# A decoder step on one core: expert scoring with four blocks per matmul, and retention samples in groups of 32 partitions

## The chip, the cores and the metric

The kernel runs on one core of one Trainium2 chip. The metric is the time of one execution on the device in microseconds (us). Names: TensorE (PE, matmuls; its weight loads are PEld), VectorE (DVE), ScalarE (ACT), GpSimd (POOL), SyncE (SP, which only issues DMAs here). Data lies in SBUF (128 partitions); matmuls write PSUM (eight banks of 512 fp32 per partition).

## The reference

One layer of a hybrid decoder, for 512 prompt tokens and 8 samples of 8 new tokens each (576 tokens, width 2048). Cut to what the change touches:

```python
def retention_chunk(q, k, v, s, log_gamma):          # s: state (B, H, dk, dv)
    ...
    inner = jnp.einsum('bhid,bhjd->bhij', q, k) * decay[None]
    o = (jnp.einsum('bhij,bhjv->bhiv', inner, v)
         + jnp.einsum('bhid,bhdv->bhiv', q, s) * xi[None, :, :, None])
    s_new = (s * jnp.exp(log_gamma * C)[None, :, None, None]
             + jnp.einsum('bhjd,bhjv->bhdv', k * zeta[None, :, :, None], v))
    return o, s_new
...
def retention_mixer(q, k, v, gate, pos, s0, ret_norm_g):   # 4 heads of 256
    ...
    o = (o - mu) * lax.rsqrt(var + NORM_EPS)
    return jax.nn.silu(gate) * (o * ret_norm_g), s_new
...
def peer(h, peer_wq, peer_subkeys, peer_u, peer_v):  # 8 heads, 16384 experts, 16 chosen of each
    ...
        u = jnp.take(peer_u, expert, axis=0)
        act = jax.nn.gelu(jnp.einsum('thkd,td->thk', u, xb), approximate=False)
        vv = jnp.take(peer_v, expert, axis=0)
        return jnp.einsum('thk,thkd->td', g * act, vv)
```

Around it: the input projection, causal pooling of the other half of the channels, the output projection, attention over 256 memory tokens per sequence, and a final norm.

## The kernel before

Every large product is made of three fp32r matmuls, high x high, high x low and low x high. A piece of weights (128 x 1024 fp32, 512 KB) arrives in a raw buffer by a DMA from SP; ScalarE rounds it into the high part of a slot of `WS` (`high`, `high2`, line 896), GpSimd subtracts to get the low part (`low_part`, line 404), TensorE uses it. `WS` has four slots; semaphores count the chain: `raw0` to `raw3`, `hi_done`, `split_done`, `used`. The tokens' parts lie in `HL`. `projection` (line 521) has the weights stationary and tokens moving (288 or 320 columns). Order on each engine is the order of the code; there is no scheduler.

**Retention** (`retention`, four heads; the last outside the loop). A head has eight projection blocks of two slots each (`head_block`, blocks 0 to 7); work on the previous results stands between them. After block 5 TensorE forms the prompt scores (line 626) and one 64 x 64 matrix of the samples (line 629); after block 6 the outputs. There, for each half of the head's channels, the four prompt tiles (line 639), the samples' inner part (line 641), and per sample and half of dk a matmul with a 128 x 128 piece of the sample's state stationary and its eight tokens moving (line 645). Then the prompt state (line 650). The new sample states are formed with the masked keys `KM` (64 partitions, one mask per sample): `state(b)` (line 660) writes bank 4 or 5, VectorE adds it to the decayed state (line 1494) and frees the bank. Two stand before block 7, the others between its k blocks. The means over the channels (line 669) stand before block 7, the variances (line 683) behind it. ScalarE copies the outputs out of PSUM, stores the states, takes the root, and only then loads the next head's tables and states and evacuates its block 0. In the last head block 7 is the first part of the output projection (`out_early`, 14 of 16 k blocks), for which ScalarE and VectorE split the mixed activations meanwhile (`split_early`, `lows`, line 1423).

**Expert scoring.** 320 tokens are scored later, against all experts. For the last 256 tokens `tokens_first` (line 793) runs inside the loop over the eight query heads: each iteration has two query projections, then the scores of 1/8 of the experts, 8 pairs of blocks of 128 experts. The tokens (`HLG`) are stationary, two expert blocks move at once: 256 columns, 96 matmuls to a pair. Slots are refilled in halves of 512 columns (`used_q`, `hi_q`, `split_q`; GpSimd's half subtractions are line 428), and the loads come in the order 0, 2, 1, 3. ScalarE applies Gelu to 512 columns (`gelu_tokens`, line 1223) and stores them to `gelg`, from which GpSimd later gathers. VectorE meanwhile selects the top 16 of the query head (lines 1581 to 1625). After it a later stage scores the other tokens and multiplies by v, with rows of `vE` gathered.

## Time and profile before

| | us |
|---|---|
| median of 3 runs | 4879.75 |
| lowest, highest | 4876.03, 4882.84 |
| the profiled execution, as timed | 4868.53 |
| its span in the trace | 4866.4 |
| TensorE busy | 4551.1 |
| GpSimd busy | 3099.6 |
| VectorE busy | 2297.8 |
| ScalarE busy | 1584.6 |

The retention heads lie between about 390 and 980 us of the span, the query projections with the scoring of 256 tokens between 1750 and 2737 us. A row of the timeline gives the start, the length and the engine, the line, the operation, "written <- read" by the program's names, the shape, how many instructions were merged, and in brackets how long the engine was idle before and what ended that. Matmul times include the way through the array, so neighbouring ones overlap: the pace is read from the start of one row to that of the next, or from a count over a stretch. An fp32 matmul (not fp32r) shows as two instructions. [...]

### The profile page before, as it was taken

Reading aid. Unit: us, or ns where it says so; the run is one execution under the profiler, and the core shown is the slowest. Engines: PE = TensorE matmul, PEld = TensorE weight load, DVE = VectorE, ACT = ScalarE, POOL = GpSimd, SP = SyncE. Lnnn points to the kernel's source line nnn. Section 1 sums busy time; section 2 is a strip of 40 time slices with the busy share of each in tenths; the row PEclk is TensorE's granted clock in tenths of the full one; section 3 lists DMA queues with packets and bytes.
Section 4 is the critical chain, followed back from the end, with each engine's and each line's share of the span. In section 5 each row is a group of like instructions: output and inputs, shape, how many; then the busy total and the mean of one; then the engine's idle time right before and its main releaser. Section 6 shows DMA issues by size and latency. Waiting matters only on the chain.

```text
span 4866.4 us, 82443 instructions
## 1 busy us (share of the span) xinstructions
PE 4551.1 (94%) x31875; PEld 4401.3 (90%) x31875; DVE 2297.8 (47%) x3074; ACT 1584.6 (33%) x2194; POOL 3099.6 (64%) x1782
## 2 busy tenths in 40 slices
PE   7999999998998989999999888799999999999997
PEld 7799988897887979999999888799999999999997
DVE  3721322423001154444444555466666666666656
ACT  4422111222222134444444454233333333333333
POOL 6833222243221447777777766799999899998864
PEclk9999999999998999999999988899999999999998
DMA  6553222332555245555555556999999899999954
GB/s 217 191 93 103 97 97 87 107 120 105 186 200 177 83 146 173 173 173 172 173 174 174 156 158 176 334 342 344 344 342 346 322 347 341 341 344 357 347 187 140
DMA packets 466611, 1032.95 MB, mean 212 GB/s; under 512 B 136944, under 2 KB 227184, under 8 KB 433648
## 3 DMA queue, kind: packets, MB, share of 16 engines
q1 hardware_dynamic: 216080, 590.67, 36.1%
q0 software_dynamic: 45056, 268.60, 14.3%
q10 hardware_dynamic: 205280, 170.84, 10.8%
q8 instruction: 152, 2.49, 0.2%
q14 instruction: 43, 0.35, 0.0%
HBM read 935.25 MB, written 94.73 MB: 212 GB/s over the span
## 4 chain that ended last, share of the span: by engine, by line
issue 38%; POOL 35%; PE 18%; DMA 4%; DVE 2%; ACT 1%; another core or an unknown queue 1%; POOLq 0%; ACTq 0%; SPq 0%; DVEq 0%
POOL WS L404 23%; PE PS L864 9%; POOL WS L428 8%; PE PS L521 5%; POOL ROWS L450 3%; PE PS L793 2%; DMA AR<-in_vE 2%; POOL AR L440 2%; PE PS L839 2%; ACT WS L896 1%; DMA RAW<-in_vE 1%; DMA gel<-AR 0%; DVE AR L1371 0%; POOL AR L450 0%
## 5 line engine op out<-in xcount | busy, mean ns | idle before, releaser
L521 PE MATMUL PS<-HL,WS 128*128 128x288 f32 (+2 forms) x16896 | 2426.7, 304 | 127.3 <-DVE HL L1408 33.9
L521 PEld LDWEIGHTS PS<-HL,WS 128*128 128x128 f32 x16896 | 2371.5, 192 | 163.0 <-issue 110.4
L404 POOL TENSOR_TENSOR WS<-RAW,WS 128x1024 fp32r<-128x1024 f32 x490 | 1200.6, 2463 | 1354.7 <-ACT WS L896 1350.7
L864 PE MATMUL PS<-WW,WS 128*128 128x320 f32 x6144 | 941.8, 315 | 79.6 <-POOL WS L404 62.9
L864 PEld LDWEIGHTS PS<-WW,WS 128*128 128x128 f32 x6144 | 922.2, 192 | 98.6 <-issue 79.2
L896 ACT ACTIVATE WS<-RAW 128x1024 fp32r<-128x1024 f32 (+1 forms) x714 | 628.1, 919 | 1011.3 <-PE PS L521 360.2
L793 PE MATMUL PS<-WS,HL 128*128 128x256 f32 x6144 | 740.5, 283 | 0.0
L793 PEld LDWEIGHTS PS<-WS,HL 128*128 128x128 f32 x6144 | 738.3, 192 | 0.0
L1677 DVE SCALAR_TENSOR_TENSOR PS<-ROWS,AR,PS 128x2048 f32<-128x2048 f32 x206 | 483.8, 2349 | 77.1 <-DMA ROWS<-in_vE,AR 76.8
L404 POOL TENSOR_TENSOR WS<-AR,WS 128x1024 fp32r<-128x1024 f32 x182 | 452.3, 2489 | 42.6 <-ACT WS L896 41.7
L404 POOL TENSOR_TENSOR WS<-CS,WS 128x1024 fp32r<-128x1024 f32 x144 | 347.4, 2413 | 187.0 <-ACT WS L896 185.2
L1692 DVE TENSOR_TENSOR AR<-AR,PS 128x320 f32<-128x320 f32 x512 | 248.6, 486 | 435.7 <-PE PS L864 423.8
L896 ACT ACTIVATE WS<-CS 128x1024 fp32r<-128x1024 f32 (+1 forms) x256 | 223.0, 871 | 495.4 <-PE PS L864 257.2
L896 ACT ACTIVATE AR<-PS 128x512 f32<-128x512 f32 (+11 forms) x255 | 172.7, 719 | 560.5 <-PE PS L521 295.4
L428 POOL TENSOR_TENSOR WS<-RAW,WS 128x512 fp32r<-128x512 f32 x224 | 304.6, 1389 | 16.8 <-ACT WS L896 15.6
L896 ACT ACTIVATE WS<-AR 128x1024 fp32r<-128x1024 f32 (+1 forms) x294 | 259.8, 888 | 129.1 <-PE PS L521 53.3
L440 POOL DMA_INDIRECT AR<-gelg,AR x256 | 249.4, 974 | 70.6 <-issue 65.2
L1581 DVE MAX8 AR<-AR 128x8 f32<-128x128 f32 (+1 forms) x120 | 30.1, 324 | 488.8 <-ACT AR L896 487.6
L450 POOL DMA_INDIRECT ROWS<-in_vE,AR x206 | 200.2, 972 | 32.0 <-issue 25.5
L1232 ACT ACTIVATE AR<-PS 128x320 f32<-128x320 f32 x128 | 56.7, 443 | 449.9 <-PE PS L521 379.8
L1665 DVE TENSOR_TENSOR AR<-AR 128x320 f32<-128x320 f32 x128 | 193.9, 1566 | 0.1
L1677 DVE SCALAR_TENSOR_TENSOR PS<-AR,PS 128x2048 f32<-128x2048 f32 x50 | 117.6, 2353 | 115.4 <-DMA AR<-in_vE,AR 115.4
(160 smaller groups left out, 2883.3 us busy)
## 6 DMA issues: line engine op xcount, KB each, us to landing
RAW<-in_uT SPq DMA_DIRECT2D x256, 512.0 KB
RAW<-in_w_lin SPq DMA_DIRECT2D x218, 512.0 KB
CS<-in_uT SPq DMA_DIRECT2D x128, 512.0 KB
AR<-in_uT SPq DMA_DIRECT2D x128, 512.0 KB
RAW<-in_vE SPq DMA_DIRECT2D x128, 512.0 KB
CS<-in_vE SPq DMA_DIRECT2D x64, 512.0 KB
AR<-in_vE SPq DMA_DIRECT2D x64, 512.0 KB
AR<-in_w_lin SPq DMA_DIRECT2D x46, 512.0 KB
```

Source lines behind the costliest of these rows:

```text
L404: pool.tensor_tensor(WS[:, k, 1, :], raw(k, many, late), WS[:, k, 0, :].bitcast(F32), ALU.subtract)\
L428: pool.tensor_tensor(WS[:, k, 1, half], raw(k, True, True)[:, half], WS[:, k, 0, half].bitcast(F32), ALU.subtract).then_inc(S["split_done" ...
L440: pool.indirect_dma_start(out=GA[:, c, k:k + 1], out_offset=None, in_=values, in_offset=at(EL[:, c, k:k + 1]))\
L450: pool.indirect_dma_start(out=ROWS[b], out_offset=None, in_=rows, in_offset=at(VI[:, c, r:r + 1]))\
L521: ins = mm(to, WS[:, slot + hf, wp, k * P:(k + 1) * P], x, start=first and (wp, xp) == (0, 0), stop=last and wp == 1, skip_group_check=True)
L793: ins = mm(to, HLG[:, c, xp, kb, :], WS[:, 2 * hf:2 * hf + 2, wp, k * P:(k + 1) * P], start=(kb, c, wp, xp) == (0, 0, 0, 0), stop=kb == KB ...
L839: ins = mm(bank(4 + q % 2, P, off=P * k), BB[:, q % 2, k, :], AA[:, q % 2, k, :], start=True, stop=True, skip_group_check=True)
L864: ins = mm(bank(2 + d % 2, ND), WS[:, 2 * (q % 2) + b, vp, 512 * e + P * d4:512 * e + P * (d4 + 1)], W[:, 2 * b + e, wp, :], start=(b, e, ...
L896: copy = lambda out, in_, **kw: act.activation(out, in_, ACT.Identity, **kw)
L1665: tt(gi, gi, PP[:, e // 2, :, e % 2, :], ALU.mult).then_inc(S["w_done"], 1)
L1677: stt(ACC, ROWS[b], GA[:, c, r:r + 1], ACC, ALU.mult, ALU.add).then_inc(S["row_done"], 1)
L1692: tt(X[:, d, 0:ND], X[:, d, 0:ND], bank(2 + d % 2, ND), ALU.add).then_inc(S["v_free"], 1)
```

## The change

Two independent parts.

**Scoring.** `tokens_first` takes four blocks of 128 experts at once: 512 moving columns, 96 matmuls to four blocks, each into a whole bank (`c` picks the bank). A load brings, for four blocks, two of the 16 k blocks: pieces of 1 KB (`load_quarters`, eight loads to four blocks). A slot feeds 12 matmuls. The handing on in halves is gone: slots are copied and subtracted whole (`low_parts`), each with its own `used`. Gelu works on 1024 columns, and the store has half as many, twice as large.

**Retention.** Samples 4r + q (r = 0, 1) lie in group q of 32 partitions, eight tokens at 8r, the rest zeros: `VSP`, `KSP`, `QSP`, `QXZ`, `INZ`. Scores of the samples are four matmuls of 32 x 32 per half. Outputs are formed token-first: `QXZ` (32 columns) stationary, the state's 256 columns moving, four column groups at a time into bank 6; the result is copied by ScalarE (`OSR`) and turned by two transposes. They now stand ahead of the prompt's outputs. `KM` needs two masks instead of eight (`ZM`), on 128 partitions; new states are formed in two rounds of four samples, each sample in its own group of 32 rows and its own bank (`state_round`). No state and no mean stands before block 7: the rounds come after its k blocks 1 and 5, the means after 9 (`states`). ScalarE loads the masks once by 16 small DMAs (8 rows each) before the pooling stage, and VectorE clears the padded tiles there.

```diff
-            def load_u(half, n, count, order=(0, 1, 2, 3)):
...
+            def load_quarters(quad, n):
+
+                for k in range(8):
+                    sp.wait_ge(S["split_done"], free(n + k, 4))
+                    sp.dma_start(raw(k % 4, True, True).rearrange("p (e w) -> p e w", e=4),
+                                 uT.rearrange("(b x) p w -> x b p w", x=2)[k // 4, bass.ds(4 * quad, 4), :, 256 * (k % 4):256 * (k % 4 + 1)]
+                                 .rearrange("b p w -> p b w")).then_inc(S[f"raw{k % 4}"], 16)
...
-                                pool.tensor_tensor(WS[:, k, 1, half], raw(k, True, True)[:, half], WS[:, k, 0, half].bitcast(F32),
-                                                   ALU.subtract).then_inc(S["split_done" if at else "split_q"], 1)
+            with pool.Fori(0, EH * H_HQ // 4) as i:
+                low_parts(i * 4 + H_WQ, late=True)
...
-                    ins = mm(bank(7, TS, TS, 256), RK[:, c, TP:T], RQ[:, c, TP:T], start=c == 0, stop=c == 1)
+                    for q in range(4):
+                        ins = mm(PS[32 * q:32 * q + 32, 512 * 7 + 256:512 * 7 + 288], KSP[:, c, q, :], QSP[:, c, q, :],
+                                 start=c == 0, stop=c == 1, skip_group_check=True)
...
+                for k in range(2):
+                    for r in range(2):
+                        for q in range(4):
+                            mm(PS[32 * q:32 * q + 32, 512 * 6:512 * 6 + RD], QXZ[:, k, r, q, :], SST[:, 4 * r + q, k, :],
+                               start=(k, r) == (0, 0), stop=False, skip_group_check=True)
+                for q in range(4):
+                    ins = mm(PS[32 * q:32 * q + 32, 512 * 6:512 * 6 + RD], INZ[:, q, :], VTOK[:, 4, :],
+                             start=False, stop=True, skip_group_check=True)
+                ins.then_inc(S["so_done"], 1)
...
-                    for b in range(SB):
-                        for k in range(2):
-                            ins = mm(bank(6, SQ, off=TS * c + SQ * b), SST[:, b, k, P * c:P * (c + 1)],
-                                     QX[:, k, SQ * b:SQ * (b + 1)], start=False, stop=k == 1, skip_group_check=True)
...
+                pe.wait_ge(S["so_copied"], h + 1)
+                for c in range(2):
+                    ins = pe.transpose(bank(6, P, off=RD + P * c), OSR[:, P * c:P * (c + 1)], IDENT)
+                ins.then_inc(S["so_turned"], 1)
...
+                def state_round(r):
                     for c in range(2):
-                        ins = mm(bank(4 + b % 2, RD, off=RD * c), KM[:, b, P * c:P * (c + 1)], VTOK[0:TS, 4, :],
-                                 start=True, stop=True, skip_group_check=True)
+                        for q in range(4):
+                            rows = slice(32 * q, 32 * q + 32)
+                            ins = mm(bank(4 + q, RD, off=RD * c), KM[rows, r, P * c:P * (c + 1)], VTOK[rows, 4, :],
+                                     start=True, stop=True, skip_group_check=True)
                     ins.then_inc(S["ks_mm"], 1)
...
                 def states(k2):
-                    if k2 + 2 < SB:
-                        state(k2 + 2)
+                    if k2 == 0:
+                        pe.wait_ge(S["km_done"], h + 1)
+                        pe.wait_ge(S["o_evac"], h + 1)
+                        pe.wait_ge(S["spr_evac"], h + 1)
+                        state_round(0)
+                    elif k2 == 2:
+                        pe.wait_ge(S["sst_new"], h * SB + 4)
+                        state_round(1)
+                    elif k2 == 4:
+                        pe.wait_ge(S["sst_new"], h * SB + 8)
+                        means()
...
+            def tokens_first(h, j, quarters):
...
+                for q in quarters:
+                    pe.wait_ge(S["split_done"], n + split(q))
+                    for k in range(2):
+                        for c in range(2):
+                            for wp, xp in ((0, 0), (0, 1), (1, 0)):
+                                experts = WS[:, q % 4, wp, :].rearrange("p (e k n) -> p k e n", e=4, k=2)[:, k]
+                                ins = mm(tiles(bank(2 * (j % 2) + c)), HLG[:, c, xp, 2 * q + k, :], experts,
+                                         start=(q, k, wp, xp) == (0, 0, 0, 0), stop=(q, k, wp) == (7, 1, 1),
+                                         skip_group_check=True)
+                    ins.then_inc(S["used"], 1)
...
+                act.wait_ge(S["so_done"], h + 1)
+                copy(OSR, bank(6, RD)).then_inc(S["so_copied"], 1)
                 act.wait_ge(S["o_done"], h * 2 + 1)
                 copy(OT[:, :, 0:TP], PS[:, 2048:3072].rearrange("p (c n) -> p c n", c=2))
...
+                for q in range(8):
+                    act.wait_ge(S["used"], n + used(q + 1))
+                    high(n + (q + 4), q % 4, late=True)
...
+                act.activation(GOG[:, e].rearrange("p s n -> p (s n)"), PS[:, 1024 * e:1024 * (e + 1)], ACT.Gelu)\
+                    .then_inc(S["lin_evac"], 1)
```

TensorE's queue in the last head, from the samples' part of the outputs into the block behind them. Before (639 to 645 outputs, 650 prompt state, 660 sample states, 669 means, 521 the projection):

```order
L641 MATMUL PS<-AR 128x64
L645 MATMUL PS<-AR 128x8 x16
L650 MATMUL PS<-AR 128x256 x8
L660 MATMUL PS<-AR 128x256 x4
L669 MATMUL PS<-AR,ONES 128x288 x4
L521 MATMUL PS<-HL,WS 128x288 x12
L660 MATMUL PS<-AR 128x256 x2
```

After (649 and 652 the samples' outputs, 657 the prompt's, 662 transposes, 666 prompt state, 674 a round of states, 681 means, 529 the projection):

```order
L649 MATMUL PS<-AR 32x256 x16
L652 MATMUL PS<-AR 32x256 x4
...
L657 MATMUL PS<-AR 128x128
L662 MATMUL PS<-CST,AR 128x128 x2
L666 MATMUL PS<-AR 128x256 x8
L529 MATMUL PS<-HL,WS 128x288 x12
L674 MATMUL PS<-AR 128x256 x8
L529 MATMUL PS<-HL,WS 128x288 x24
L674 MATMUL PS<-AR 128x256 x8
L529 MATMUL PS<-HL,WS 128x288 x24
L681 MATMUL PS<-AR,ONES 128x288 x4
```

The samples' outputs moved ahead of the prompt's, and all states and the means moved into the block.

ScalarE's queue at the end of the last head, from the last pieces of `split_early` (943 and 958 its loads of the mixed activations, 896 and 911 the copies out of `CS` and `AR` into `HL`) to the copies of the outputs. Before:

```order
L943 DMA CS<-mixT 128x576 [waits lo_ready]
L896 ACTIVATE HL<-CS 128x576 [waits in_z0]
L896 ACTIVATE HL<-CS 128x576 [waits in_z1]
L896 ACTIVATE AR<-PS 128x2x512 [waits o_done]
L896 ACTIVATE AR<-PS 128x2x64
L896 ACTIVATE AR<-PS 128x512 [waits o_done]
L1083 DMA out_nret_p<-AR 128x2x256 [waits spr_evac]
```

After:

```order
L958 DMA CS<-mixT 128x576 [waits lo_ready]
L911 ACTIVATE HL<-CS 128x576 [waits in_z0]
L911 ACTIVATE HL<-CS 128x576 [waits in_z1]
L911 ACTIVATE AR<-PS 128x256 [waits so_done]
L911 ACTIVATE AR<-PS 128x2x512 [waits o_done]
L911 ACTIVATE AR<-PS 128x2x32 [waits so_turned]
L911 ACTIVATE AR<-PS 128x2x32
L911 ACTIVATE AR<-PS 128x512 [waits o_done]
L1120 DMA out_nret_p<-AR 128x2x256 [waits spr_evac]
```

The copy that waits for `so_done` (the samples' rows) is new and stands behind the whole loop; TensorE's transposes (line 662) wait for it. The loop's own order did not change.

TensorE's queue in the scoring, inside an iteration (788 and 806 count the slots). Before:

```order
L793 MATMUL PS<-WS,HL 128x256 [waits split_q]
L793 MATMUL PS<-WS,HL 128x256 x23
L788 REGISTER_ALU
L793 MATMUL PS<-WS,HL 128x256 [waits split_done]
L793 MATMUL PS<-WS,HL 128x256 x23
```

After:

```order
L806 REGISTER_ALU
L811 MATMUL PS<-WS,HL 128x512 [waits split_done]
L811 MATMUL PS<-WS,HL 128x512 x11
L806 REGISTER_ALU
L811 MATMUL PS<-WS,HL 128x512 [waits split_done]
L811 MATMUL PS<-WS,HL 128x512 x11
```

Each wait now covers one slot with 12 matmuls of 512 columns, where it covered halves of two slots with 24 matmuls of 256.

## Rows read from the trace of the kernel before

**Rows 1.** The page, part 1: busy us, share of the span, instructions.

```profile
PE 4551.1 (94%) x31875; PEld 4401.3 (90%) x31875; DVE 2297.8 (47%) x3074; ACT 1584.6 (33%) x2194; POOL 3099.6 (64%) x1782
```

**Rows 2.** Groups by line: shapes, count | busy us, mean ns | idle before.

```profile
L793 PE MATMUL PS<-WS,HL 128*128 128x256 f32 x6144 | 740.5, 283 | 0.0
```

**Rows 3.** Windows: length, busy us (instructions) of the engines, clock, DMA, GB/s; two of one line.

```profile
core 0: us, PE busy (x) PEld busy (x) DVE busy (x) ACT busy (x) POOL busy (x), PEclk, DMA share, GB/s
2144.00:2263.00 119.00, 116.87 (x957) 116.70 (x956) 51.81 (x144) 48.02 (x77) 94.50 (x64) 1.00 0.55 177
...
1920.00:1960.00 40.00, 40.00 (x336) 40.00 (x335) 1.00 0.62 202
...
150.00:220.00 70.00, 70.00 (x311) 57.96 (x310) 1.00 0.64 211
```

**Rows 4.** Windows over the middle of heads 0, 1, 2 and 3, TensorE.

```profile
476.66:501.46 24.80, 24.80 (x118) 0.79 0.16 54
627.94:651.14 23.20, 23.20 (x118) 0.85 0.16 57
775.86:800.77 24.91, 24.91 (x119) 0.79 0.16 53
911.61:941.43 29.82, 29.82 (x116) 0.66 0.50 149
```

**Rows 5.** Timeline of TensorE in head 1: start, length, instructions.

```profile
627.94 2.32 PE L639 MATMUL PS<-AR 128*128 128x512 f32 x8
...
630.55 3.74 PE L645 MATMUL PS<-AR 128*128 128x8 f32 x32
...
641.60 5.87 PE L650 MATMUL PS<-AR 128*128 128x256 f32 x16
...
651.14 1.96 PE L521 MATMUL PS<-HL,WS 128*128 128x288 f32 x12
653.03 1.13 PE L660 MATMUL PS<-AR 64*128 64x256 f32 x4
654.09 1.84 PE L521 MATMUL PS<-HL,WS 128*128 128x288 f32 x12
...
668.26 3.45 PE L521 MATMUL PS<-HL,WS 128*128 128x288 f32 x24
```

**Rows 6.** Timeline of GpSimd and VectorE beside line 554 and in the scoring.

```profile
184.69 5.27 POOL L404 TENSOR_TENSOR WS<-AR,WS 128x1024 fp32r<-128x1024 f32 x2
...
2195.20 7.75 POOL L428 TENSOR_TENSOR WS<-RAW,WS 128x512 fp32r<-128x512 f32 x4 [0.41 <-ACT WS L896]
2195.57 4.78 DVE L1617 TENSOR_TENSOR AR<-AR,CST 128x1280 f32<-128x1280 f32 x2
```

**Rows 7.** Timeline of a load in the scoring; time to landing of the key cache (line 329).

```profile
2208.88 0.33 SPq L298 DMA_DIRECT2D AR<-in_uT  x1
...
2213.75 0.63 ACT L896 ACTIVATE WS<-AR 128x512 fp32r<-128x512 f32 x1 [1.43 <-DMA AR<-in_uT]
...
DMA to landing us min/median/max: 3.9/8.2/10.5
```

**Rows 8.** Timeline of TensorE in the attention, column groups of 32.

```profile
1253.17 1.93 PE L719 MATMUL PS<-AR 128*32 128x256 f32 x32
```

**Rows 9.** Timeline of head 1: state updates, and TensorE's wait in the next head.

```profile
648.56 1.61 DVE L1494 SCALAR_TENSOR_TENSOR AR<-AR,PS 128x512 f32<-128x512 f32 x2 [31.59 <-PE PS L660]
...
704.52 7.67 PE L521 MATMUL PS<-HL,WS 128*128 128x288 f32 x46 [3.13 <-POOL WS L404]
```

**Rows 10.** Timeline of the last head, TensorE and ScalarE.

```profile
911.61 4.06 PE L639 MATMUL PS<-AR 128*128 128x512 f32 x8 [1.90 <-DVE AR L1487]
...
930.89 0.68 ACT L896 ACTIVATE HL<-CS 128x576 fp32r<-128x576 f32 x1 [0.97 <-DMA CS<-mixT]
...
932.04 5.71 PE L650 MATMUL PS<-AR 128*128 128x256 f32 x16
...
960.27 2.10 PE L683 MATMUL PS<-AR,ONES 128*128 128x288 f32 x8
```

**Rows 11.** Timeline of ScalarE before the first pooling evacuation.

```profile
244.35 1.38 ACTq L1009 DMA_DIRECT2D AR<-in_spoolT  x2
247.70 2.01 ACT L896 ACTIVATE WS<-RAW 128x1024 fp32r<-128x1024 f32 x2 [4.34 <-PE PS L521]
```

More of the change, by code:

```diff
@@ L66 @@
 QT = NQ - LAG // 2
[L67 to L68 removed]
+UPQ = NQ // EH
+H_HQ = 4 + 8 * UPQ
 H_P = H_WQ + H_HQ * EH
@@ L363, in _, with load_u @@
             load_lin(H_MO + 4, H_WQ)
-            def load_u(half, n, count, order=(0, 1, 2, 3)):
+            def load_u(half, n, count):
                 for k in range(count):
-                    load(n + k, k % 4, uT[bass.ds(half + (k - k % 4 + order[k % 4]), 1)], late=True)
+                    load(n + k, k % 4, uT[bass.ds(half + k, 1)], late=True)
+            def load_quarters(quad, n):
[4 more added lines that the diff above has]
+                                 .rearrange("b p w -> p b w")).then_inc(S[f"raw{k % 4}"], 16)
             def load_v(i, n):
@@ L815, in _ @@
                 ins.then_inc(S["sk_done"], 1)
-                tokens_first(h, 0, 1)
-                for j in range(1, UPP):
-                    for hf in range(2):
-                        tokens_first(h, j, hf)
+                tokens_first(h, 0, range(2, 8))
+                for j in range(1, UPQ):
+                    tokens_first(h, j, range(8))
             pe.wait_ge(S["soft_done"], 1)
@@ L1023, in _ @@
             act.wait_ge(S["x_added"], 1)
+            for b in range(SB):
+                r, q = b // 4, b % 4
+                rows = slice(32 * q + SQ * r, 32 * q + SQ * (r + 1))
+                act.dma_start(ZM[rows], tabs[:, SQ * b:SQ * (b + 1), T_ZETAS + b - r:T_ZETAS + b - r + 2].rearrange("h p n -> p h n"))\
+                    .then_inc(S["in_pad"], 16)
+                act.dma_start(DECP[rows, :, SQ * r:SQ * (r + 1)],
+                              tabs[:, SQ * b:SQ * (b + 1), T_DECS + SQ * b:T_DECS + SQ * (b + 1)].rearrange("h p n -> p h n"))\
+                    .then_inc(S["in_pad"], 16)
             for g in range(GROUPS):
@@ L1076, in retention @@
                     split_early(mixT, Z_OUT, OUT_EARLY, (0, 0, 0), LO_OUT)
+                act.wait_ge(S["so_done"], h + 1)
+                copy(OSR, bank(6, RD)).then_inc(S["so_copied"], 1)
                 act.wait_ge(S["o_done"], h * 2 + 1)
                 copy(OT[:, :, 0:TP], PS[:, 2048:3072].rearrange("p (c n) -> p c n", c=2))
-                copy(OT[:, :, TP:T], bank(6, 2 * TS).rearrange("p (c n) -> p c n", c=2)).then_inc(S["o_evac"], 1)
+                act.wait_ge(S["so_turned"], h + 1)
+                turned = bank(6, RD, off=RD).rearrange("p (c q x) -> p c q x", c=2, q=4)
+                for r in range(2):
+                    ins = copy(by_token(OT, r), by_group(turned, r))
+                ins.then_inc(S["o_evac"], 1)
                 act.wait_ge(S["o_done"], h * 2 + 2)
@@ L1247, in _ @@
                     high2(h * H_HQ + (H_WQ + 2 * c + 4), 2 * c, late=True)
-                for j in range(UPP):
+                for j in range(UPQ):
                     gelu_tokens(h, j)
```

184 lines of the change are left out of this document (77 added, 107 removed), and 2 rows, old and new, of the table names.

## The prediction

> **What bounds the kernel now.** I read the profile page first, then the groups of instructions by line, then the timeline of the two places that the change touches, then windows with the granted clock. TensorE is busy for 4551.1 of 4866.4 us [rows 1], so a change pays where it shortens TensorE's own queue, and only if nothing else is already waiting beside it.
>
> Place one is the scoring of the last 256 tokens against all experts (line 793): 6144 matmuls with 256 moving columns, 740.5 us in all, no idle time before them, 120.5 ns each [rows 2]. The clock is granted in full there; in the same stretch GpSimd is busy 94.5 of 119 us, VectorE 51.8, ScalarE 48.0, and the DMA engines stand at 0.55 [rows 3]. TensorE is the bound, GpSimd the next.
>
> Place two is the middle of each of the four retention heads. From the first output matmul to the start of block 7 it takes 24.8, 23.2 and 24.9 us in heads 0 to 2 and 29.8 us in the last, at a mean clock of only 0.79, 0.85, 0.79 and 0.66 [rows 4]. The reader should see in the timeline that 32 matmul instructions with 8 columns take 3.74 us, twice per head, that is 117 ns each although there is next to nothing to stream, and that line 650 behind them runs its 16 instructions in 5.87 us [rows 5]. Line 639 shows what such fp32 work costs at full clock: 8 instructions with 2 x (512+384+256+128) = 2560 columns start to end in 2.32 us, some 2.25 without the tail, 0.88 ns per column. Line 650 (256 columns each) would be 16 x 225 ns = 3.6 us at that rate. So the small matmuls cost twice: themselves, and the clock of what follows.
>
> **Part A, four blocks moving.** 6144 matmuls of 256 columns become 3072 of 512. The nearest row is line 554, the same form (HL stationary, WS moving, fp32r, 12 matmuls to a slot): 311 in 70 us at full clock [rows 3]. A window counts those in flight at both edges, some two, so 70/309 = 226.5 ns. Counted alike, line 793 has 40/334 = 119.8 ns, by its group 120.5. The saving is 3072 x (239.6 to 241.0 - 226.5) = 40 to 45 us; I take **42 us**. The fixed part of a matmul is thus about 13 ns at both widths, and half of those parts go.
>
> [...]
>
> What must keep up with it: per slot (a 128x1024 piece of weights) TensorE now needs 12 x 226.5 = 2.72 us. GpSimd's subtraction of a full slot took 5.27 us for two beside line 554, 2.64 each, while TensorE ran through [rows 6]. In the scoring, with VectorE busy 37.88 of 40 us, 28 half slots took 36.98 us [rows 3], 1.32 each, again 2.64 a slot. ScalarE's copy of a slot is 2.01 us for two [rows 11]; with one Gelu over as many columns per 8 slots, taken alike, it works 9 of 21.8 us. GpSimd falls behind only beside line 1617 of VectorE: four half slots took 7.75 us there [rows 6], 3.9 us per full slot, but line 1617 lasts 4.78 us per head, so some 1.5 us are lost. Four slots exist, and a slot freed by TensorE is ready after 1.0 + 2.64 + some 0.3 us of signals (an estimate) = 4.0, against 3 x 2.72 = 8.2 until it is wanted: 4 us of cover. Cost taken: 0; without the cover it would be 1.5 to 2.5 us per head.
>
> Loads: the same bytes in pieces of 1 KB instead of 4 KB. One uT load was issued at 2208.88 and waited for until 2213.75, 4.9 us [rows 7]. A buffer goes round in landing + 4.0 us and four of them must turn in 4 x 2.72 = 10.9, so a landing may take 6.9 us. The nearest row with 1 KB pieces is the key cache, 3.9 to 10.5 us, median 8.2, but with eight loads queued behind each other [rows 7]; here one or two are. I take 5 us, hidden. The end of the stage (last copy, Gelu, then softmax) moves by less than 1 us; taken as 0.
>
> **Part B, heads 0 to 2.** The 64 eight-column instructions and 4 of line 641 become 40 with 32-column weights and 256 moving columns, four column groups side by side. The attention has just this: 32 instructions in 1.93 us, some 55 ns each [rows 8]. So 40 x 55 + 0.2 = 2.4 us. Then line 639's work at full clock 4.5 us, two turned blocks 0.25 us, line 650's 3.6 us, and 0.5 us for switching between tilings (the 0.33 us gaps seen in the weight loads' queue there, an estimate). The wait for the copy of the sample rows is hidden behind the 4.5 us of prompt matmuls: ScalarE has an evacuation and two slot copies first, some 3 us (an estimate from the 1.0 us of a copy).
>
> States: before, 8 times four instructions, two of them ahead of block 7, the other six each 1.06 us inside it [rows 5]. After, two rounds of 16 instructions on 32-row groups. No row shows row groups side by side; bounds are the 55 ns of column groups (0.9 us a round) and 220 ns each in turn (3.5 us). I take the lower, since the four column groups did overlap with the same pairs of fp32 passes and the rounds write four banks: 2 x 0.9 + 0.4 = 2.2 us. VectorE needs 1.61 us for two updates [rows 9], so 3.2 us for four plus 0.3 us of signals, against 24 matmuls of block 7, 3.3 us [rows 5]: 0.3 us of waiting twice, 0.6. The means (1.83 us, unchanged) then stand after kb 9; the squares they lead to take 2.8 us on VectorE against 4.9 us of matmuls left: hidden. The 16 instructions for the sample scores instead of 4: +0.5 us (bounds 0.4 to 1.5, by 55 and 117 ns).
>
> Sum after: 2.4 + 4.5 + 0.25 + 3.6 + 0.5 + 2.2 + 0.6 + 0.5 + 1.8 = 16.4 us. Before: 23.2 + 6 x 1.06 = 29.6 us in head 1, 31.2 and 31.3 in heads 0 and 2. Saved 14.8 + 13.2 + 14.9 = 42.9 us. The next head waits for slots (3.13 us on line 404 in [rows 9]) at the end of a chain that begins with block 7's end: states out, square root, b, mixT. That chain moves with block 7 and keeps its length, but ScalarE has one more copy of 64 columns in it, 0.3 us per head: **-42 us**.
>
> **Last head.** ScalarE is held by the loop that splits mixT: its last copy there starts at 930.89, while TensorE started the output matmuls at 911.61 [rows 10]. They will now end near 919, and the new wait for the copy of the sample rows stands behind that loop: TensorE idles some 13 us and goes on at about 932, where line 650 starts now [rows 10]. So the output part gains nothing here, and the clock falls again. From 932.04 to 960.27 [rows 10] are 28.2 us; after: transposes 0.5, line 650 at a low clock 6.2, rounds 2.2, waits 0.6, means 1.8, 84 matmuls of the block 11.6 = 22.9. **-5 us.**
>
> **Other edits.** ScalarE issues 16 tiny loads before the first pooling evacuation, and VectorE clears 1408 columns (1.4 us) before them. Two such issues took 1.38 us and ScalarE waited 4.34 us after them [rows 11]; at 0.4 us each it ends 5 us late, and GpSimd's first slot of the third projection is ready 4 us before it is wanted. Cost 0; at 0.7 us each, 1 us. VectorE's masks (one instruction instead of 8) and small copies lie in its idle time.
>
> **Sum.** 42 + 42 + 5 = 89, about 90 us. The profiled execution took 4868.5 us, so its like would be 4778.5; the median, 4879.75, is 11 us above it, and I forecast 4790.
>
> **Rivals.**
> R1, row groups run one after another: 3.5 instead of 0.9 us per round, 2.6 x 2 x 4 = 21 us more, 4811. For it: no row shows them together. Against: the column groups. [...] Chance 12%.
> R2, GpSimd sets the pace while VectorE is busy: 2.5 us per head, 20 us, 4810. For it: 2.64 against 2.72 us per slot is thin. Against: line 793 has no idle time [rows 2] although GpSimd worked 36.98 of 40 us beside it [rows 3]. 12%.
> R3, the clock stays low in the middle of a head although the small matmuls are gone: lines 639 and 650 twice as long, 8.1 us x 3 = 24, 4814. 8%.
> R4, the fixed part is small at 512 columns: 35 us more gained, 4755. 5%.
> R5, **slower than before**: the 1 KB pieces land too late. A slot then takes (landing + 4.0)/4. All gain is lost from 697 + 90 = 787 us for 256 slots, 3.07 us per slot, a landing of 8.3 us; at the 10.5 us of [rows 7] a slot takes 3.6 us and the kernel some 5020. For it: the key cache's median of 8.2. Against: only one or two loads are in flight, and v's 2 KB pieces feed the last stage. 3%.
> R6, a gain eaten elsewhere in whole (a wait that I have not seen at the start of a head): within 0.2%, 4880. 3%. My forecast and its neighbours hold the remaining 57%.
>
> **How the numbers follow.** Forecast 4790, its own spread 4775 to 4805 (A 40 to 45, the QK and round bounds, 4 us of scatter between runs). The range takes in R1 to R3, alone or two of them in part: 4768 to 4825; outside are R4, R5, R6 and pairs in full. About 0.2% (10 us) is what a measurement can tell from no change: faster 94%, same 3%, slower 3%.
>
> **What would show it.** Scoring matmuls at 226 to 229 ns with no idle, GpSimd near 92% there; landing of uT under 7 us. In heads 0 to 2 the middle takes about 11.5 us at a clock of 1.00, a round about 1.1 us. In the last head TensorE idle some 13 us behind ScalarE. Wrong would be: scoring matmuls waiting on line 404's subtraction or ScalarE on DMA (R2, R5), 3.5 us per round (R1), a clock below 0.9 in heads 0 to 2 (R3).

## The result: 4759.81 us, 8 us below the range

The changed kernel takes 4759.81 us (median of 4 runs, 4754.19 to 4767.14) against 4877.89 us before (4 runs, 4875.43 to 4882.84): a ratio of 0.9758, 95% interval 0.9741 to 0.9775. 118 us were gained; forecast were 90, and a range that ended at 4768. The profiled execution took 4756.82 us, its span is 4754.9 us, 111.5 less than the span of before.

The page of the changed kernel, part 1 (beside [rows 1]), and the scoring's group by line (beside [rows 2]):

```profile
PE 4437.2 (93%) x28747; PEld 4178.8 (88%) x28747; DVE 2364.5 (50%) x3080; ACT 1561.5 (33%) x1954; POOL 3059.0 (64%) x1558
...
L811 PE MATMUL PS<-WS,HL 128*128 128x512 f32 x3072 | 700.1, 389 | 0.0
```

TensorE is busy 114 us less and still the bound (93% of the span). The scoring's group fell from 740.5 to 700.1 us. To see where the 111.5 us are, take stages between the same events of TensorE's timeline in both kernels:

| stage, from | before | after | change |
|---|---|---|---|
| retention: 363.23 / 363.86, last pooling matmuls | 615.9 | 558.4 | -57.5 |
| 979.10 / 922.27, after the last head's wait for VectorE | 565.3 | 563.3 | -2.0 |
| 1544.41 / 1485.57, attention's output projection | 209.3 | 204.4 | -4.9 |
| scoring of 256 tokens: 1753.70 / 1689.94 | 990.9 | 936.1 | -54.8 |
| dense stage (scores of the other tokens): 2744.62 / 2626.03 | 316.7 | 324.0 | +7.3 |
| 3061.35 / 2950.06, weighting by v, to TensorE's last matmul | 1779.7 | 1779.5 | -0.2 |

The changed kernel starts this table 0.6 us later, and 25.4 us follow it in both. A stage's time is not the same in every record of the same code: over all traces of this document the retention stage took 614.1 to 622.5 us in four records of its old code and 554.8 to 560.1 in eight of the new one, so its gain is known to some 4 us. The timeline of TensorE in head 1 (beside [rows 5]) and windows over the middles of heads 0 to 3 (length, busy us and instructions of PE, PEld, DVE, ACT, POOL, clock as TensorE's granted share of full speed, DMA share, GB/s; beside [rows 4]):

```profile
609.10 1.93 PE L649 MATMUL PS<-AR 128*32 128x256 f32 x32
610.85 0.61 PE L652 MATMUL PS<-AR 128*32 128x256 f32 x8
611.40 4.58 PE L657 MATMUL PS<-AR 128*128 128x512 f32 x16
615.82 0.38 PE L662 MATMUL PS<-CST,AR 128*128 128x128 f32 x2
616.03 3.62 PE L666 MATMUL PS<-AR 128*128 128x256 f32 x16
619.30 1.93 PE L529 MATMUL PS<-HL,WS 128*128 128x288 f32 x12
621.16 1.15 PE L674 MATMUL PS<-AR 32*128 32x256 f32 x16
622.24 3.44 PE L529 MATMUL PS<-HL,WS 128*128 128x288 f32 x24
```

```profile
477.24:487.44 10.20, 10.20 (x75) 7.12 (x75) 0.00 (x0) 4.18 (x8) 4.66 (x2) 1.00 0.30 103
609.10:619.30 10.20, 10.20 (x75) 7.12 (x75) 0.00 (x0) 4.18 (x8) 4.66 (x2) 1.00 0.31 103
741.29:751.49 10.20, 10.20 (x76) 7.12 (x75) 0.00 (x0) 4.18 (x8) 4.66 (x2) 1.00 0.30 103
860.90:887.72 26.82, 12.48 (x74) 8.65 (x75) 10.46 (x14) 9.60 (x16) 0.00 (x0) 0.75 0.51 141
```

The middle fell from 23.2 to 24.9 us to 10.20 with no gap in it, the clock is granted in full (1.00, before 0.79 to 0.85), and a round of states takes 622.24 - 621.16 = 1.08 us (start of its row to start of the next). The last head is the exception, and its timeline (brackets: idle before, and what ended it) shows why:

```profile
863.20 4.58 PE L657 MATMUL PS<-AR 128*128 128x512 f32 x16
882.12 0.69 PE L662 MATMUL PS<-CST,AR 128*128 128x128 f32 x2 [14.34 <-ACT AR L911]
882.60 5.47 PE L666 MATMUL PS<-AR 128*128 128x256 f32 x16
```

The scoring in windows of the same form (PE, clock, DMA, GB/s), and TensorE at the start of a query head, before and after:

```profile
1850.00:1900.00 50.00, 50.00 (x222) 1.00 0.68 209
1965.00:2015.00 50.00, 50.00 (x223) 1.00 0.68 209
```

```profile
2119.81 7.36 PE L793 MATMUL PS<-WS,HL 128*128 128x256 f32 x60
2128.87 3.32 PE L521 MATMUL PS<-HL,WS 128*128 128x320 f32 x23 [1.70 <-issue]
```

```profile
1924.75 4.70 PE L811 MATMUL PS<-WS,HL 128*128 128x512 f32 x20
1929.29 2.97 PE L529 MATMUL PS<-HL,WS 128*128 128x320 f32 x21
```

With two matmuls in flight at the edges, 50/220.5 = 226.8 ns per matmul of 512 columns, as line 554 had. And something that the prediction did not speak of: before, TensorE stood idle 1.5 to 2.1 us ahead of seven of the eight query heads, released by "issue" (nothing that the profile shows). The summary of what line 521 waited for, over that stretch of the kernel before, gives the sum; after, there is no such idle time:

```profile
  issue: 12.3, 7
```

### The profile page after: what moved, and what is told of

Its sections match the earlier page's. It is cut to its first block, busy times and chain, and to the rows that moved or that the text cites. A ratio compares the mean times of both kernels' runs of the same rounds, so it can differ in the third digit from the quotient of the medians.

```text
span 4754.9 us, 75671 instructions
## 1 busy us (share of the span) xinstructions
PE 4437.2 (93%) x28747; PEld 4178.8 (88%) x28747; DVE 2364.5 (50%) x3080; ACT 1561.5 (33%) x1954; POOL 3059.0 (64%) x1558
## 3 DMA queue, kind: packets, MB, share of 16 engines
q8 instruction: 86, 1.41, 0.1%
## 4 chain that ended last, share of the span: by engine, by line
PE 37%; issue 26%; POOL 26%; DMA 4%; DVE 3%; another core or an unknown queue 2%; ACT 1%; ACTq 0%; POOLq 0%; DVEq 0%; SPq 0%
POOL WS L424 21%; PE PS L811 15%; PE PS L529 12%; PE PS L879 9%; POOL ROWS L458 3%; DMA AR<-in_vE 2%; POOL AR L448 2%; PE PS L854 1%; DMA RAW<-in_vE 1%; ACT WS L911 1%; DVE AR L1427 1%; DVE AR L1401 1%; DMA gel<-AR 0%; POOL AR L458 0%
## 5 line engine op out<-in xcount | busy, mean ns | idle before, releaser
L424 POOL TENSOR_TENSOR WS<-RAW,WS 128x1024 fp32r<-128x1024 f32 x602 | 1477.1, 2466 | 1296.0 <-ACT WS L911 1291.3
L911 ACT ACTIVATE WS<-RAW 128x1024 fp32r<-128x1024 f32 x602 | 617.8, 1055 | 994.9 <-PE PS L529 351.0
L811 PE MATMUL PS<-WS,HL 128*128 128x512 f32 x3072 | 700.1, 389 | 0.0
L811 PEld LDWEIGHTS PS<-WS,HL 128*128 128x128 f32 x3072 | 575.6, 188 | 118.9
L424 POOL TENSOR_TENSOR WS<-AR,WS 128x1024 fp32r<-128x1024 f32 x238 | 600.4, 2526 | 45.8 <-ACT WS L911 44.8
L424 POOL TENSOR_TENSOR WS<-CS,WS 128x1024 fp32r<-128x1024 f32 x200 | 492.5, 2462 | 199.7 <-ACT WS L911 198.1
L911 ACT ACTIVATE AR<-PS 128x512 f32<-128x512 f32 (+9 forms) x271 | 175.7, 690 | 612.3 <-PE PS L529 379.7
L911 ACT ACTIVATE WS<-CS 128x1024 fp32r<-128x1024 f32 x200 | 211.6, 1058 | 415.6 <-PE PS L879 260.6
L911 ACT ACTIVATE WS<-AR 128x1024 fp32r<-128x1024 f32 x238 | 249.9, 1055 | 202.8 <-PE PS L811 93.0
L1659 DVE TENSOR_TENSOR AR<-AR 128x256 f32<-128x256 f32 x80 | 203.2, 2610 | 0.3
```

The costliest lines, as they stand in the source:

```text
L424: pool.tensor_tensor(WS[:, k, 1, :], raw(k, many, late), WS[:, k, 0, :].bitcast(F32), ALU.subtract)\
L811: ins = mm(tiles(bank(2 * (j % 2) + c)), HLG[:, c, xp, 2 * q + k, :], experts, start=(q, k, wp, xp) == (0, 0, 0, 0), stop=(q, k, wp) == (7 ...
L911: copy = lambda out, in_, **kw: act.activation(out, in_, ACT.Identity, **kw)
L1659: ins = tt(v, v, SIF[:, c, t, :].unsqueeze(1).to_broadcast([P, TOPK, TOPK]), ALU.mult)
```

## The experiments

The runs were made on several chips of the same kind; each is compared with the kernel before, timed on the same chip. The kernel before took 4811 to 4812 us on three of them and 4876 on the fourth, 4878 where the result above was measured, so only ratios and stages of the trace are compared across chips.

**Each part alone.** The kernel before with the scoring's hunks of the diff, then with the retention's.

> Only the scoring part (512 moving columns, quarter loads). Theory now: a head's iteration of the scoring loop falls from 121.9 to 114.9 us, 5.2 by the wider matmuls and 1.75 because the gap of 1.5 to 2.1 us before the next iteration's first matmul disappears; the stage 1750 to 2740 us loses about 55 us, the kernel about 55 (4823 against 4878). The retention's milestones stay as before. If the pace of the plain projection between 1554 and 1740 us (133.3 ns per matmul before, 130.0 after) belongs to the retention edit, it stays 133.3 here; if it is scatter between loads of a program, it may be either. Rival from the prediction: only 42 us gained, the gap stays.

> Only the retention part. Theory: the gain up to the first matmul behind the last head is 57 us (3 x about 17 and some 6 in the last head), 4820 against 4878; the scoring keeps its gap of 1.5 to 2.1 us per iteration and its 120 ns per matmul. If the two parts add up, the gains of this and of the scoring alone sum to about 118 us; if the 7 us lost between 2626 and 2950 us of the changed kernel come from the scoring part, this kernel doesn't show them and the sum is larger.

Measured: 4749.67 us for the scoring (ratio 0.9866, 0.9849 to 0.9882) and 4755.10 us for the retention (0.9874, 0.9855 to 0.9893), beside 4812.39 before: 62.7 and 57.3 us, 120 together, against 118 for both on the other chip, so the parts add up within the intervals. The scoring stage took 936.1 us in the first, to a tenth what it takes with both parts, and the gaps were gone; the retention stage took 560.1 us in the second, and the gaps in the scoring were there. That stage took 998.1 us in the second, 7 more than in the kernel before, with 14.8 us of "issue" in it for 12.3 (more on this below). The stage from 1544 us on took 208.8 us in the first and 204.3 in the second, which would have put its 5 us down to the retention part; later records of the changed kernel as it stands took that away again (below).

**Does the gap belong to the jump?** TensorE's loop over the query heads, in the kernel before, written out:

```diff
-            with pe.Fori(0, EH) as h:
+            for h in range(EH):
```

> The kernel before, with TensorE's loop over the eight query heads written out (no jump back). Theory that the gap before each iteration's first matmul is the price of the jump: seven gaps of 1.5 to 2.1 us go, 12 us less (4866 against 4878), scoring matmuls still 120 ns. Rival, the gap is a wait for data (slots, banks): it stays, 0 us.

Measured: 4794.02 us, ratio 0.9961 (0.9949 to 0.9973). The scoring stage fell from 990.9 to 977.1 us, no "issue" in it. It is the jump. (The medians differ by 18 us; the stage accounts for 14 of them, the rest is unexplained.)

**Why the wide matmuls remove it.** My theory was that TensorE's queue holds enough long matmuls to cover what a jump costs. (How many it holds no run shows; the 16 in the next text is my guess.) First only the last slot of a head was made narrow again, then the last four blocks (`if j == UPQ - 1`), then all.

```diff
-                                ins = mm(tiles(bank(2 * (j % 2) + c)), HLG[:, c, xp, 2 * q + k, :], experts,
+                                parts = (slice(0, 2), slice(2, 4)) if (j, q) == (UPQ - 1, 7) else (slice(0, 4),)
+                                for part in parts:
+                                    ins = mm(tiles(bank(2 * (j % 2) + c))[:, part], HLG[:, c, xp, 2 * q + k, :], experts[:, part],
```

> The changed kernel, with only the last slot of each head's scoring split into 24 matmuls of 256 columns. By width alone it costs 12 x 13.3 ns x 8 = 1.3 us. Theory that the jump is hidden behind the matmuls queued at its time (some 16 x 227 ns = 3.6 us, against 16 x 120 = 1.9 us): the gap of about 1.7 us comes back seven times, 13 us slower than the changed kernel (4773). Rival, the gap went because the loop's code is shorter or lies elsewhere: no gap, 1 to 2 us slower (4761).

> Only the last four blocks of each head's scoring narrow: 192 matmuls of 256 columns for 96 of 512. By width 8 x 96 x 13.3 ns = 10 us. If TensorE's issue gets ahead by more than the 24 short matmuls tried before and loses its lead within 192 (23 us), the gap returns: 10 + 12 = 22 us slower than the changed kernel; if the gap depends on the whole loop or on the hand-over, 10 us.

> The changed kernel's loads, slots and hand-over, with every matmul of the scoring split into two of 256 columns. By width: 6144 x 120.0 against 3072 x 226.7 ns, 41 us slower than the changed kernel. If the gap at the jump back is there when the matmuls in front of it are short (TensorE's queue cannot get far ahead at 120 ns each), it returns, 7 x 1.75 = 12 us more, 53 in all, as before. If the gap belonged to the old hand-over in halves (its waits), it does not: 41.

(The last two leave out a part of the sums; number, shape and waits of the matmuls are as meant.) The scoring stage took 937.4, 946.3 and 997.5 us against 936.1: 1.3 and 10.2 us more are the width alone, without a gap. Only with all matmuls narrow are the gaps back, 1.5 to 3.7 us, some of them put down to "issue" and some to GpSimd. In total 4690.98, 4703.95 and 4753.30 us; the changed kernel beside the last two:

> The changed kernel itself, as a reference beside the next three. In the kernels run so far the dense stage (the later scoring, from the transposes of the gates to its last block) took 256 to 258 us, where the two records of before and after took 317 and 324 with short stalls of TensorE's instruction issue. If those stalls belong to the chip and not to the code, this run takes 257 us there and about 4694 in all; if to the code of the changed kernel, 324 us and 4760.

It took 4695.29 us, ratio 0.9758 again. So 192 narrow matmuls before the jump don't bring the gap back: the theory of the queue fell. That left the length of the code: with all matmuls narrow the loop's body is as long as before. Two runs tell length from pace. One makes the body twice as long at the new pace (two heads in one turn):

> The changed kernel, with two query heads written out in the body of TensorE's scoring loop: three jumps back instead of seven, and a body about as long in code as twice the changed one, longer than that of the kernel before. If the gap at a jump depends on the length of the body, it shows before the first matmul of every second head: three of 1.5 to 2.1 us, 5 us slower than the changed kernel. If it depends on how far TensorE's issue is ahead (matmuls of 227 ns let it run ahead, of 120 ns not), there is none: 0.

Measured: 4768.04 us, ratio 0.9777 (0.9761 to 0.9793); the scoring stage 939.0 us, 2.9 more than in the changed kernel, where I expected 5. The timeline has one gap of 0.7 us at each of the three jumps and nothing between. Two stand before the first matmul of the turn, at 1931.14 and 2392.83; the other one comes 25 matmuls after it:

```profile
1931.14 4.12 PE L529 MATMUL PS<-HL,WS 128*128 128x320 f32 x29 [0.68 <-issue]
```

```profile
2161.07 3.51 PE L529 MATMUL PS<-HL,WS 128*128 128x320 f32 x25
2165.30 4.91 PE L529 MATMUL PS<-HL,WS 128*128 128x256 f32 x35 [0.73 <-issue]
```

The other shortens the body at the old pace:

```diff
-                for j in range(1, UPP):
-                    for hf in range(2):
-                        tokens_first(h, j, hf)
+                with pe.Fori(0, (UPP - 2) // 2) as i:
+                    for jj in range(2):
+                        for hf in range(2):
+                            tokens_first(h, jj + 1, hf, i)
+                for hf in range(2):
+                    tokens_first(h, UPP - 1, hf)
```

> The kernel before, its matmuls still of 256 columns, but blocks 1 to 6 of the eight pairs of a head in an inner loop of three turns on TensorE: the code of a head's iteration shrinks from 980 matmul rows to 596, about what the changed kernel has, and there are two jumps more in each head. If the length of the code behind a jump decides, the gap before each head goes and the inner jumps (192 matmuls) have none: the scoring stage 12 us shorter than before, about 978 us. If the pace decides (matmuls of 120 ns leave no lead), every jump has its gap of 1.5 to 2.1 us: 23 in place of 7, the stage 25 us longer than before.

Measured: the scoring stage 977.1 us, exactly as long as with the loop written out, no "issue" before any line 521, in spite of two jumps more per head; 4793.41 us, ratio 0.9962 (0.9951 to 0.9973). **The length of the body decides.** Matmuls in the body of a turn and gap at its jump: 192 and none (the inner loop here), 586 and none (here and in the changed kernel), 682 and none (last four blocks narrow), 970 and 1.5 to 2.1 us (before; all narrow, up to 3.7), 1172 and 0.7 us (two heads). The pace may have a part in the size, since the longest body has wide matmuls and the smaller gap; that was not tried apart.

The traces show what goes with the length. The profile names DMA queue q8 "instruction"; its packets have 16 KiB each (page, part 3: 152 packets, 2.49 MB before). They follow TensorE's code: editing its loop alone changes the count for the whole kernel from 152 before to 143 (2.34 MB) with the loop written out and 86 (1.41 MB) with the short body, while the edits of ScalarE's and VectorE's code below leave the changed kernel's 86 as it is. Over the scoring stage (packets, MB, share of the 16 engines) of the kernel before, of the changed kernel, and of two heads in a turn:

```profile
q8 instruction: 71, 1.16, 0.4%
```

```profile
q8 instruction: 5, 0.08, 0.0%
```

```profile
q8 instruction: 46, 0.75, 0.4%
```

The short body has 5 too, the one with its last four blocks narrow 6, all of them in the first turn: in the other seven turns none comes. For the longer bodies packets come in every turn, after the first turn's eight (ten with two heads) nine (before), ten (all narrow, and the retention part alone) or twelve (two heads). With the loop written out 62 come and TensorE has no such idle time, so packets without a jump stopped TensorE nowhere here; the gaps stand only where a jump back and packets in every turn come together. The packet at the jump before 2128.87 was started at 2125.99 and took 1.15 us; TensorE was idle from 2127.17. Where ten packets come in a turn the stage takes 6 to 7 us more than where nine do (998.1 us, or 997.5, against 990.9), for the same 970 matmuls: second gaps of 0.3 to 1.4 us then follow some jumps, 25 matmuls behind them. Why ten come there and nine before is not shown.

So bodies for which five or six packets came (98 KB at most) ran without a gap and brought in nothing after the first turn; those of nine (147 KB) and more had both. Where the limit lies between them no run shows, nor that the packets cause the gap.

**The 8-column matmuls.** The kernel before without line 645:

```diff
-                    for b in range(SB):
-                        for k in range(2):
-                            ins = mm(bank(6, SQ, off=TS * c + SQ * b), SST[:, b, k, P * c:P * (c + 1)],
-                                     QX[:, k, SQ * b:SQ * (b + 1)], start=False, stop=k == 1, skip_group_check=True)
```

> The kernel before without the 8-column matmuls (line 645); the samples' part of the outputs from the states is left out. Theory that they cost twice: 7.5 us per head themselves, and the clock of lines 639 and 650 behind them. Then line 650 falls from 5.9 to 3.3 us and the clock of the middle from 0.79-0.85 to 1.00: some 12 us per head in heads 0 to 2, 8 in the last, 44 to 48 us in all. Rival, the clock falls for another reason (the fp32 form, the waits): 7.5 us per head, 30 us in all, line 650 still 5.9 us.

One execution: 4836.87 us against 4876.02. TensorE's timeline of head 1, and the window over its middle:

```profile
614.59 2.32 PE L639 MATMUL PS<-AR 128*128 128x512 f32 x8
...
619.91 3.72 PE L646 MATMUL PS<-AR 128*128 128x256 f32 x16
...
627.32 1.95 PE L521 MATMUL PS<-HL,WS 128*128 128x288 f32 x12
```

```profile
614.59:627.32 12.73, 12.73 (x55) 9.20 (x53) 1.50 (x2) 4.33 (x6) 4.65 (x2) 1.00 0.32 103
```

From 23.20 at clock 0.85 to 12.73 at 1.00: 10.5 us. In the kernel before the first batch of 8-column matmuls took 3.6 us to the start of the next row and the second, with the clock falling, 4.8 (its row has 4.90 us, which [rows 5] doesn't show): 8.4 us are the matmuls themselves. The other 2.1 are the clock behind them, on line 650 (here 646), from 5.8 to 3.7. They do cost twice, though the second cost is less than I took it for. The retention stage gained 36 us, less than I expected, since in the last head the time turned into a wait of 10.8 us for ScalarE, as it did in the changed kernel.

**Row groups.** The changed kernel, all four samples of a step on the first group:

```diff
-                            rows = slice(32 * q, 32 * q + 32)
+                            rows = slice(0, 32)
```

> The changed kernel with all four matmuls of a round's step on the first 32 partitions, instead of each on its own 32; the new states of three samples out of four are wrong by that. Theory that a round takes 1.08 us (16 instructions, 67 ns each) because four groups of rows work side by side: on one group they run in turn, at 107 ns or more each, 1.9 to 3.5 us a round, 7 to 19 us slower in all. Rival, a matmul of this kind takes 67 ns anyway: 1.08 us a round, no change.

TensorE's timeline of head 1, the first round and what follows:

```profile
628.53 3.72 PE L674 MATMUL PS<-AR 32*128 32x256 f32 x16
632.17 3.44 PE L529 MATMUL PS<-HL,WS 128*128 128x288 f32 x24
```

One execution took 4788.19 us. 3.64 us a round instead of 1.08, 228 ns per instruction instead of 68, and a retention stage of 584.2 instead of 558.4 us. Four groups of 32 rows work side by side, 3.4 times as fast as one (256 columns of fp32). The 107 ns that I expected as the least are what 256 more columns cost a matmul in the scoring (226.8 - 120).

**The last head's idle time.** ScalarE's copies put between the pieces of its split loop (behind pieces 3, 5 and 8), then also VectorE's first four state updates behind its piece 11:

```diff
-                    split_early(mixT, Z_OUT, OUT_EARLY, (0, 0, 0), LO_OUT)
+                    split_early(mixT, Z_OUT, OUT_EARLY, (0, 0, 0), LO_OUT,
+                                then=lambda b: {3: samples_out, 5: outputs, 8: prompt_state}.get(b, lambda: None)())
...
-                    lows(Z_OUT, LO_OUT, 0, OUT_EARLY)
+                    lows(Z_OUT, LO_OUT, 0, 11)
...
                 for b in range(SB):
+                    if not more and b == 4:
+                        lows(Z_OUT, LO_OUT, 11, OUT_EARLY)
```

> The changed kernel, with ScalarE's copies of the last head's outputs put between the pieces of its split loop instead of behind it. Theory that the 14.3 us of TensorE's idle time before line 662 are ScalarE's queue: the idle goes; TensorE then runs the first k blocks of the output projection until VectorE's updates (behind its own part of the loop) hold it for the second round of states, at about 883 us. 6 to 10 us faster than the changed kernel. Rival, something else is late next (the split itself, k block by k block): 0 to 3 us.

> The kernel with ScalarE's copies between the splits, and now also VectorE's first four state updates between its pieces of the same loop (after piece 11 of 14). The wait of 6.9 us before the second round of states goes; the k blocks behind it then wait for VectorE's last pieces instead, some 2.7 us later than now. 4 to 7 us faster than with ScalarE's copies alone, 14 to 18 us faster than the changed kernel. Rival, the end of the split loop decides all the same: 0 to 2 us.

TensorE's timeline of the last head with both moved:

```profile
866.58 0.38 PE L662 MATMUL PS<-CST,AR 128*128 128x128 f32 x2
...
873.48 1.15 PE L674 MATMUL PS<-AR 32*128 32x256 f32 x16 [1.48 <-ACT AR L911]
...
879.69 1.15 PE L674 MATMUL PS<-AR 32*128 32x256 f32 x16 [1.67 <-DVE AR L1549]
...
908.44 5.26 PE L529 MATMUL PS<-HL,WS 128*128 128x288 f32 x24 [5.40 <-DVE HL L1466]
```

And with ScalarE's copies alone:

```profile
868.24 0.38 PE L662 MATMUL PS<-CST,AR 128*128 128x128 f32 x2
...
884.98 2.09 PE L674 MATMUL PS<-AR 32*128 32x256 f32 x16 [6.87 <-DVE AR L1547]
```

The 14.34 us are gone; with the copies alone 6.87 us of idle time come up at the second round, behind VectorE's part of the loop. The retention stage takes 553.0 and 545.0 us against 554.8 to 560.1 in the records without the moves. So the copies alone are hardly clear of that spread, both moves together are. In total 4683.63 us on the chip where the changed kernel took 4695.29, and 4747.81 us (ratio 0.9734, 0.9718 to 0.9750). The last pair, once more beside each other:

> The changed kernel as a reference beside the next. The stage from 1485 to 1690 us took 204 or 209 us in the records so far, the same kernel both: it may be either here. Ratio to the kernel before 0.976.

> The kernel with ScalarE's copies and VectorE's updates between the pieces of the split loop, again, with more rounds: the retention stage 13 us shorter than in the changed kernel beside it (545 against 558 us), the ratio to it 0.997 to 0.998.

4689.33 and 4681.68 us, ratios 0.9748 (0.9729 to 0.9767) and 0.9730 (0.9711 to 0.9748); the retention stages 558.8 and 545.5 us. The five executions of each do not overlap (4686.42 to 4696.08 and 4677.34 to 4682.94). The records of the stage differ by 13.3 us, the medians by 8; which stages of the other executions made up the rest no trace shows. One source of such scatter is known: the stage from 1485 us on took 204.4 us in one record of the changed kernel and 208.8 and 208.9 in two others. So those 5 us, in the table above too, belong to no edit. They are a pace, as the same window of that stage in the first and the second of these records shows (us, TensorE busy, its instructions, clock, DMA share, GB/s):

```profile
1600.00:1650.00 50.00, 50.00 (x386) 1.00 0.26 85
1600.00:1650.00 50.00, 50.00 (x377) 1.00 0.25 84
```

With two in flight at the edges that is 130 or 133 ns for each matmul of 288 columns, at full clock. Why a stage runs at one or the other is open. By its ratio this is the fastest version that was run; with the copies alone it was 0.9735 (0.9719 to 0.9752), too near to tell apart by time.

**The dense stage.** It took 256 to 258 us in every record from three of the chips, and 317 to 324 on the fourth and in the first two records. The same kernel, windows over that stage, where the result above was measured and on another chip:

```profile
2626.03:2950.06 324.03, 269.44 (x1705) 254.97 (x1706) 162.12 (x254) 146.71 (x159) 196.71 (x146) 0.86 0.56 158
```

```profile
2631.50:2889.60 258.10, 233.63 (x1706) 231.09 (x1706) 162.24 (x254) 149.70 (x159) 196.69 (x146) 0.96 0.70 200
```

The instructions are the same. What differs is "issue", once in each turn of the loop: single matmuls with 0.2 to 1.7 us between them, and a lower clock over the stage (0.86 against 0.96). The waits of TensorE in the stage, before, and in the changed kernel where it took 258 us:

```profile
PE PS L839 <- issue: 17.8, 23, 1.7
PE PS L521 <- issue: 17.7, 28, 1.6
```

```profile
PE PS L529 <- POOL WS L424: 22.7, 11, 18.0
```

On the fourth chip the stage took 323.3, 317.7, 319.1 and 321.6 us in four kernels that share its code, three of them with the changed scoring. So the +7.3 us of the table is within what this stage does there for no edit's sake. Nor does it go with packets on q8: in the stretch of these stalls (2801 to 3025 us before, 2680 to 2920 after) none comes. Why that chip stalls at issue is open; no experiment was made on it.

## Where the prediction was right and where not

- **Part A's width**: forecast 42 us. The kernel before without its gaps has a stage of 977.1 us, the changed one 936.1: 41.0. 226.8 ns per matmul stood in the trace of before as line 554, and R4, the smaller fixed part, is out: no run shows its 35 us, and the fixed part came as 13 to 14 ns (twice 119.8 to 120.5, less 226.8). GpSimd kept pace (R2): no idle time on line 811. The loads did too (R5): TensorE never waited. The nearest they came is at a head's end, 6.7 to 7.4 us from issue to copy. The longest was issued at 1794.46 and copied at 1801.84, 7.4 us, above my 5 and above the 6.9 that I had allowed for every load. It is one load per head:

```profile
1794.46 0.37 SPq L384 DMA_DIRECT2D CS<-in_uT  x1
...
1801.84 1.06 ACT L911 ACTIVATE WS<-CS 128x1024 fp32r<-128x1024 f32 x1 [2.46 <-DMA CS<-in_uT]
```

- **The step that failed**: "no idle time before them" of [rows 2] was read as no idle time in the scoring. The idle time stood ahead of line 521, the first matmul of the next turn, and the windows of [rows 3] show it: TensorE busy 116.87 of 119.00 us. 12.3 us of "issue" lay on the bound engine and went; with what lies around the jumps the stage gives 13.8 us. The sum put this term at nothing. By itself it takes 4790 to 4776, still inside the range; with the 9 us of the heads below it is 4767, and the rest is the step from the profile to the median.
- **Part B, heads 0 to 2**: forecast 42, measured 57.5 - 6.1 = 51.4. The mechanism was right, each term a little too dear (and retention's stage is known to some 4 us only): the middle 10.2 instead of 11.3 us (no switching cost, and the prompt state 3.3 instead of 3.6), no wait behind the rounds (0.6), the samples' scores 0.1 cheaper instead of 0.5 dearer; 2.4 us per head. The waits of the next head on line 424 fell from 10.05 to 8.41 us in all. Rounds (2 x 1.08) and means (1.7) came as forecast; R1's bounds, 0.9 and 3.5, are what four groups and one group give, 1.08 and 3.64. R3 is out: clock 1.00.
- **Last head**, from its first output matmul to 979.10 and 922.27: forecast 5, measured 67.5 - 61.4 = 6.1; idle 14.3 us for 13.
- **From the profile to the median**: I took the profiled execution as 11 us below the median and added that. The changed kernel's profiled execution is only 3 us below its median. 8 us of the miss are this scatter, no mechanism.
- **Sum**: 9 (heads) + 14 (jump) - 1 (width) + 1 (last head) + 8 (median) is 31 for the 30 us between 4790 and 4760; 1 went where 89 was rounded to 90, and the -2.0, -4.9, +7.3 and -0.2 us of the untouched stages cancel. The measured time lies nearest to R4's 4755, but R4's mechanism did not occur: that nearness is chance.
- **A misreading without effect**: the 8-column matmuls do not take 3.74 us twice per head but 3.74 and 4.90. The sum took the middle of a head whole, so nothing hung on it.

## What to carry to other kernels

Look for idle time at the first instruction behind every loop's jump on the engine that is the bound, and not only at the group that is changed: fewer, larger matmuls also shorten the loop's body, and here a body of 970 matmuls paid some 1.8 us per jump, one of 682 nothing. The packets of the instruction queue over a loop's stretch told the two kinds apart: 5 or 6 for the bodies without a gap, 46 to 78 for those with one. Writing the loop out, or nesting a shorter one, gave the same without any other change (14 us of the scoring stage). Where an engine's new copy unblocks the bound engine, it must not stand behind a long loop on its own queue: behind it TensorE stood idle for 14 us. Here the next engine's work behind the same loop (VectorE's) had to be moved too before most of that was gained.

## What was not expected of the hardware

- A gap at a jump that depends on the length of the loop's body: none at 192 to 682 matmuls, 1.5 to 2.1 us at 970 of 120 ns (up to 3.7 in one run), 0.7 us at 1172 of 227 ns. For bodies of up to 682 matmuls five or six packets of 16 KiB came on the instruction queue, all in the first turn; for those of 970 and more nine to twelve came in every later turn.
- The same stage of 288-column matmuls at full clock runs at 130 ns each in some executions and 133 in others.
- Four groups of 32 rows with 256 fp32 columns: 68 ns per instruction, against 228 ns on one group.
- One stage, of the same instructions, 258 us on three chips and 317 to 324 on a fourth, with stalls at instruction issue.
